# HGRN gate functions regrouped around the tenth projection, and the first mLSTM scores placed ahead of the context states

## The reference, cut to what matters

```python
def _hgrn_gates(f_pre, lb):
    fp = f_pre.astype(jnp.float32)
    logf = jnp.log(lb + (1.0 - lb) * jax.nn.sigmoid(fp))
    k = (1.0 - lb) * jax.nn.sigmoid(-fp)
    return logf, k

# HGRN, per head: q = silu(q), both directions' (logf, k), v; then a chunkwise scan
#   b = cumsum(logf);  attention inside a chunk decays with exp(b_t - b_s)
#   S_new = exp(b_last) * S + (k * exp(b_last - b))^T v
#   out = rms(o) * silu(g)

# mLSTM, per head and direction, over the latents, starting from the context's final state C
#   s = (q k^T) * exp(dlog - m);  h = (w_inter * q C + s v) / max(|den|, exp(-m))
```

## Time and profile before

| what | value |
|---|---|
| median of three runs | 2908.68 us (2907.45 to 2909.07) |
| the profiled execution, its own time | 2908.8 us |
| its span | 2907.0 us |
| PE busy | 2704.5 us (93%) |
| PE weight loads busy | 2196.0 us (76%) |
| DVE busy | 1577.1 us (54%) |
| ACT busy | 1046.3 us (36%) |
| POOL busy | 558.4 us (19%) |
| mean granted clock of PE | 0.95 of full speed |

### The profile page before, as it was taken

One profiled execution on the slowest core, in us unless ns is written; L12 is line 12 of the kernel. 1 busy time (PEld: TensorE's weight loads), 2 busy tenths in 40 slices (PEclk: granted clock), 3 DMA queues, 4 the chain that ended last, 5 costly groups with the idle time before them and its releaser, 6 DMA issues.

```text
span 2907.0 us, 33020 instructions
## 1 busy us (share of the span) xinstructions
PE 2704.5 (93%) x13552; PEld 2196.0 (76%) x13552; DVE 1577.1 (54%) x2304; ACT 1046.3 (36%) x1550; POOL 558.4 (19%) x506
## 2 busy tenths in 40 slices
PE   7999999999998988988999999999788898999998
PEld 4888888878887877965888788887585564588786
DVE  4764445368667676267622554534527875353444
ACT  4212121256566553134422343423222333253333
POOL 0101010116444441000000031310104442021111
PEclk8999999999999999989999999999986789999999
DMA  7444444321111112020222333332211120222221
GB/s 286 166 180 191 152 185 171 137 113 69 48 66 48 48 69 83 23 87 1 102 101 87 132 110 135 143 131 78 90 45 71 60 79 30 87 102 87 95 96 42
DMA packets 44935, 292.66 MB, mean 101 GB/s; under 512 B 4976, under 2 KB 4976, under 8 KB 17904
## 3 DMA queue, kind: packets, MB, share of 16 engines
q1 hardware_dynamic: 42480, 280.06, 26.1%
q10 hardware_dynamic: 2304, 10.49, 0.9%
HBM read 271.65 MB, written 18.87 MB: 100 GB/s over the span
## 4 chain that ended last, share of the span: by engine, by line
PE 81%; DVE 11%; ACT 5%; issue 2%; POOL 1%; DMA 1%; DVEq 0%; SPq 0%; POOLq 0%; another core or an unknown queue 0%; ACTq 0%
PE ps L308 80%; DVE hd L1557 1%; POOL tb L2829 1%; DVE wb L2936 1%; ACT hd L1480 0%; ACT hd L1478 0%; DVE wb L2940 0%; DMA x<-in_x 0%; DVE hd L1559 0%; PE ps L1729 0%; DVE wl L909 0%; DVE x L1581 0%; ACT L1483 0%; ACT L1478 0%; PE ps L3003 0%
## 5 line engine op out<-in xcount | busy, mean ns | idle before, releaser
L308 PE MATMUL ps<-xs,wh 128*128 128x512 f32 (+1 forms) x2816 | 785.1, 366 | 13.7 <-DVE xs L943 13.6
L308 PEld LDWEIGHTS ps<-xs,wh 128*128 128x128 f32 x2816 | 508.2, 190 | 99.0 <-issue 15.7
L308 PE MATMUL ps<-xs,wl 128*128 128x512 f32 (+1 forms) x1408 | 513.0, 364 | 0.0
L308 PE MATMUL ps<-h,wh 128*128 128x512 f32 (+1 forms) x1408 | 391.1, 364 | 7.9 <-POOL h L1141 7.9
L893 DVE TENSOR_TENSOR wl<-w,wh 128x2048 fp32r<-128x2048 f32 (+4 forms) x114 | 246.9, 2167 | 255.9 <-ACT wh L887 255.7
L887 ACT ACTIVATE wh<-w 128x2048 fp32r<-128x2048 f32 (+4 forms) x114 | 203.9, 1789 | 302.0 <-PE ps L308 271.9
L308 PEld LDWEIGHTS ps<-xs,wl 128*128 128x128 f32 x1408 | 267.1, 190 | 42.2
L308 PEld LDWEIGHTS ps<-h,wh 128*128 128x128 f32 x1408 | 253.4, 189 | 51.1 <-POOL h L1141 9.6
L308 PE MATMUL ps<-h,wl 128*128 128x512 f32 (+1 forms) x704 | 255.8, 363 | 0.0
L308 PE MATMUL ps<-x1h,wh 128*128 128x512 f32 x584 | 240.4, 412 | 7.0 <-DVE x1lr L1284 3.9
L308 PE MATMUL ps<-x1h,wl 128*128 128x512 f32 x584 | 236.3, 405 | 0.0
(11 more groups left out here) (436 smaller groups left out, 4834.6 us busy)
## 6 DMA issues: line engine op xcount, KB each, us to landing
w<-in_adat SPq DMA_DIRECT2D x52, 1024.0 KB, 4.9
w<-in_f1i SPq DMA_DIRECT2D x22, 1024.0 KB, 6.6
w<-in_f2i SPq DMA_DIRECT2D x22, 1024.0 KB, 4.8
w<-in_f3i SPq DMA_DIRECT2D x22, 1024.0 KB, 4.8
s_tables<-t ACTq DMA_DIRECT2D x16, 640.0 KB, 3.0
cs<-s_tables SPq DMA_DIRECT2D x16, 640.0 KB, 3.9
w<-in_ada SPq DMA_DIRECT2D x8, 1024.0 KB, 9.1
w<-in_whf SPq DMA_DIRECT2D x8, 1024.0 KB, 4.8
```

The source lines that it names most:

```text
L308: return e.matmul(out, l, r, start=st, stop=sp)
```

## The change

Three things change; no arithmetic is removed or added.

First, a new item `gates h` holds the four forget sigmoids on ACT and the three operations on k on DVE. It stands directly ahead of `fill h, 9`. The two Ln and the four scans move into `fill h, 9`, behind the sigmoids of q and gs and behind the request for the joint table. Second, in the last head `early 0` and `1` move from steps 2 and 3 to 0 and 1, each `drain` moves up one step, and the first value weight of mLSTM, `wmv 0`, is loaded and split inside HGRN's list (split in step 12 of head 7) instead of after it. Third, the scores and the decay of mLSTM's first unit stand ahead of the context's states on PE, its DVE part ahead of the states' copies, and ACT's scan part waits for `uC` instead of the last state.

```diff
-        out = [("fill", 0, 0), ("split", value_key(0, 0))] + [("fill", 0, p) for p in (1, 3, 4, 6, 7, 8, 9, 2, 5)]
-        out += [("split", ("whf", 1, 2048))] + [("v", 0, i) for i in range(6)] + [("prep", 0, n) for n in range(LEAD)]
+        out = [("fill", 0, 0), ("split", value_key(0, 0))] + [("fill", 0, p) for p in (1, 3, 4, 6, 7, 8, 2, 5)]
+        out += [("gates", 0), ("fill", 0, 9), ("split", ("whf", 1, 2048))] + [("v", 0, i) for i in range(6)] + [("prep", 0, n) for n in range(LEAD)]
...
-                        (7, 6): [("split", ("wmq", 1, 2048))]}.get((h, i), [])
-                out += [("early", n) for n in {(7, 2): [0], (7, 3): [1], (7, 4): [2], (7, 6): [3], (7, 8): [4],
+                        (7, 6): [("split", ("wmq", 1, 2048))], (7, 12): [("split", ("wmv", 0, 2048))]}.get((h, i), [])
+                out += [("early", n) for n in {(7, 0): [0], (7, 1): [1], (7, 4): [2], (7, 6): [3], (7, 8): [4],
...
-                out += [("drain", n) for n in {(7, 7): [0], (7, 9): [1], (7, 11): [2], (7, 13): [3]}.get((h, i), [])]
+                out += [("drain", n) for n in {(7, 6): [0], (7, 8): [1], (7, 10): [2], (7, 12): [3]}.get((h, i), [])]
...
-                out += fill if i == 9 else []
+                out += [("gates", h + 1)] + fill if i == 9 and h < 7 else []
...
@@ act_hgrn
                 if p == 9:
                     w.wait_ge(*fA.at(h, "gs", "l"))
                     e.activation(SB[0], z["q"], ACT.Sigmoid).then_inc(*fA.of(h, "sq"))
                     e.activation(SB[1], z["gs"], ACT.Sigmoid).then_inc(*fA.of(h, "sg"))
                     logs(e)
+                    for j in range(2):
+                        e.activation(z[f"b{j}"], z[f"b{j}"], ACT.Ln, scale=olb[:, j, h:h + 1],
+                                     bias=lb[:, j, h:h + 1]).then_inc(*fA.of(h, "ln", j))
+            elif item == "gates":
+                for j in range(2):
+                    e.activation(z[f"k{j}"], z[f"b{j}"], ACT.Sigmoid, scale=-1.0).then_inc(*fA.of(h, "k", j))
+                    w.wait_ge(*fA.at(h, "k", j))
+                    e.activation(z[f"b{j}"], z[f"b{j}"], ACT.Sigmoid).then_inc(*fA.of(h, "b", j))
...
@@ dve_mlstm, ahead of the copies of the context's states
+        dve_decay(e, w, 0)
...
@@ pe_mlstm, behind tc2 and ahead of the wait for kw
+        w.wait_ge(*mlA.at("k", 3))
+        w.wait_ge(*mlV.at("q", 3))
+        ml_scores(e, w, 0)
+        ml_decay(e, w, 0)
...
-        w.wait_ge(*mlV.at("C", 1, 3, 1))
+        w.wait_ge(*mlV.at("uC"))
```

More of the change, by code:

```diff
@@ L1388, in sp_hgrn @@
                         load(e, w, ("wmq", u, 2048), (mlP, "q", 2 * u + 1))
+                    for u in range(2):
+                        load(e, w, ("wmv", u, 2048), (mlP, "v", u, 3))
             elif item == "v":
@@ L1773, in sp_mlstm @@
     def sp_mlstm(e, w):
-        for u in range(2):
-            load(e, w, ("wmv", u, 2048), (mlP, "v", u, 3))
         save_out(e, w, 7)
@@ L2013, in last_exp, with dve_decay @@
         return (n, i, 1 if hi - lo > 128 else 0)
+    def dve_decay(e, w, n):
+        NB, NM = NBM[n % 2]
+        b = banks("dc", n)
+        nm = cst("nmF") if UNIT[n][1] == 0 else cst("nmB")
+        w.wait_ge(*dcP.at(n))
+        if n >= 2:
+            w.wait_ge(*dcA.at(*last_exp(n - 2, 3)))
+        e.tensor_tensor(rows(NM, 4), rows(b, 4), nm.unsqueeze(1).to_broadcast([128, 4, 128]),
+                        ALU.add).then_inc(*dcV.of(n, "m"))
+        e.tensor_copy(NB, b).then_inc(*dcV.of(n, "b"))
     def dve_scan(e, w):
         split_lo1(e, w, MGK[0], mg_hi)
-        for item, n in ML:
+        for item, n in ML[2:]:
             h, j = UNIT[n]
@@ L2020, in dve_scan @@
             if item == "decay":
[L2021 to L2029, removed]
+                dve_decay(e, w, n)
             elif item == "weigh":
@@ L2061, in dve_scan, with ml_scores, ml_decay @@
                                                    op0=ALU.mult, op1=ALU.add).then_inc(*dvV.of(n, hf, "h", t))
+    def ml_scores(e, w, h):
+        PR = slice(64 * (h % 2), 64 * (h % 2) + 64)
+        for i in range(4):
+            b = banks.take(w, "sc", h, i)
+            mm(e, b, kt[PR, h // 2, 128 * i:128 * i + 128], qt[PR, h // 2, :], True, True).then_inc(*sqP.of(h, i))
+    def ml_decay(e, w, n):
+        col = 32 * UNIT[n][1] + UNIT[n][0]
+        b = banks.take(w, "dc", n)
+        mm(e, b, ident[0:64, col:col + 1].to_broadcast([64, 128]), Mr[0:64, :], True, True).then_inc(*dcP.of(n))
+        banks.give(("dc", n), (dcV, n, "b"))
     def pe_scan(e, w):
         w.wait_ge(*mlV.at("C", 1, 3, 1))
-        w.wait_ge(*mlA.at("k", 3))
-        w.wait_ge(*mlV.at("q", 3))
-        for item, n in ML:
+        for item, n in ML[2:]:
             if item == "scores":
[L2069 to L2072, removed]
+                ml_scores(e, w, n)
                 continue
@@ L2077, in pe_scan @@
             if item == "decay":
-                b = banks.take(w, "dc", n)
-                mm(e, b, ident[0:64, col:col + 1].to_broadcast([64, 128]), Mr[0:64, :], True, True).then_inc(*dcP.of(n))
-                banks.give(("dc", n), (dcV, n, "b"))
+                ml_decay(e, w, n)
             elif item == "weigh" and j == 1:
```

50 lines of the change are left out of this document (21 added, 29 removed).

## The result

The changed kernel takes 2871.2 us (median of four runs, 2870.4 to 2872.1), the kernel before, timed beside it, 2908.9 us. The ratio is 0.9871, 95% interval 0.9854 to 0.9888: 37.6 us gained, where 54.8 were forecast. The time is inside the range given, but 17 us above the value and 5 us above the band of 2847 to 2866 us that the forecast itself had. The profiled execution has a span of 2869.2 us, 37.8 less than before.

The account below looks back on a forecast made before the run. PE, busy 93% of the span, was held by seven 6.3 us waits for DVE's KS product and the slowed clock behind them. Gains of 45.5 + 3.1 + 6.2 = 54.8 us from 2908.8 gave 2854 us, range 2840 to 2876.

Parts of the forecast that it names:

- the new stall: Ahead of the next head's first fill, PE waits 2.2 us for DVE in six heads: 13.2 us lost.
- rival 6: A table load holds ACT 2.7 us, not 1.3, ahead of the scans: 16 us more, 2870 us; chance 0.01.
- rivals 2: DVE's backlog paces the head, with a new stall of 4 to 8 us: 2865 to 2889 us; chance 0.12.
- 3: No new stall at all, DVE being 2.2 us quicker than walked: saves 13 us, 2841 us; chance 0.08.
- rival 4: PE's transposes wait on something else ending nearly as late, so little is gained: 2900 to 2910 us; chance 0.02.
- rival 5: Slower kernel: half clock for most of the head behind the stall before each next head's first fill; chance 0.03.
- no fall of the clock in it: PE's clock was to hold through the 2.2 us stall ahead of the next head's first fill, costing nothing extra.
- Rival 1: The new stall also drops the clock, costing 9 to 17 us over six heads: 2863 to 2871 us; chance 0.12.
- The sign of being wrong: A head's period over 55 us would show the forecast wrong; 53 us was expected.
- (a): Last head, early 0 first: early 2 starts at T + 34.5, T ending PE's fill 9; 6.5 us lost.
- (b): Drain 0 one step earlier: PE's 4.07 us wait halves, gaining 2.0 us, plus 1.6 us of low clock.
- (c): Early split of wmv 0 saves 5.6 us of waiting and 2.0 of half clock; 2.0 returns at the ninth bank.

Follow-up runs that it names:

- Experiments 3: Changed kernel with DVE's sel 4 moved between gates and fill 9, ahead of the scans; 2858.3 us.
- 4: Kernel of experiment 3 with the next forget weight's split also moved, directly behind fill 9; 2846.0 us.
- experiment 1: Changed kernel with only its first change kept: early products, drains, first value weight and first scores back as before; 2877.9 us.
- experiment 2: Changed kernel with early 0 and early 1 back in steps 2 and 3 of the last head; 2867.7 us.
- experiment 8: Kernel of experiment 4 with early 0 in step 2, early 1 in step 0 without waiting for rows, gate weight's split two steps earlier; 2843.3 us.
- experiment 12: Kernel of experiment 4 with early 0 and early 1 back in steps 2 and 3 of the last head; 2843.5 us.
- experiment 9: Kernel of experiment 8 with head 7's forget sigmoids, Ln and scans moved into steps 7 and 8 of head 6; 2842.1 us.
- 11: Kernel of experiment 8 with DVE filling the last four of eight low rows with zeros instead of computing them; 2842.3 us.
- experiment 5: Changed kernel with its third change undone: first scores and decay behind the context's states again; 2875.8 us.

## Why the prediction came out 17 us short

Of the 17 us between forecast and result, the rows above put 10.0 on Part 1 (35.5 for 45.5), 5.1 on Part 2 (a loss of 2.0 for a gain of 3.1) and 0.6 on Part 3 (5.6 for 6.2); the 1.3 us given back behind the first output had no term.

**Part 1, removed.** Right. No transpose waits for KS, five table loads a head are two.

**Part 1, the new stall.** Its place and length were right: 2.3 us, in six heads, at `sel 4`, where 2.2 was worked out. The walk through ACT and DVE holds row by row. The timeline of ACT and then of DVE behind fill 9 of head 1, with T = 755.85:

```profile
751.41 1.28 ACT L1490 ACT_TABLE_LOAD   x1
752.70 0.85 ACT L1490 ACTIVATE hd<-hd 128x768 f32<-128x768 f32 x1
...
758.00 1.28 ACT L661 ACT_TABLE_LOAD   x1
759.29 1.95 ACT L1479 ACTIVATE hd<-hd,small 128x768 f32<-128x768 f32 x2
```

```profile
760.36 1.23 DVE L1551 TENSOR_TENSOR_SCAN hd<-cst,hd 128x512 f32<-128x512 f32 x1 [1.57 <-ACT hd L1479]
...
763.59 1.03 DVE L1553 TENSOR_TENSOR_SCAN hd<-cst,hd 128x256 f32<-128x256 f32 x1
...
766.27 2.65 DVE L909 TENSOR_TENSOR wl<-w,wh 128x2048 fp32r<-128x2048 f32 x1
768.84 0.72 DVE L1603 COPY_PREDICATED at<-m,ps 128x512 f32<-128x512 uint8 x1
```

Scans from T + 4.5 (4.6 worked out), `sel 4` from T + 13.0 to 13.7 (13.5). The next function starts 1.29 us after either table load. The Trainium skill, page ScalarE: Activation LUTs, section "What ACT_TABLE_LOAD costs", gives the load itself about 1283 ns, with which these rows agree, and a drain of 1380 ns on top of it, which no row here shows; rival 6 is out. So are rivals 2 and 3 (the stall is 2.3 us, neither 4 to 8 nor nothing), rival 4 (no transpose waits) and rival 5 (the clock is back at 1.00 within 4 us).

**The step that failed: "no fall of the clock in it".** Rival 1 is what happened. The clock fell at all six stalls of 2.3 us: each of the six stretches of 5 us around them has a mean clock of 0.66, which is (1 - 0.66) x 5 = 1.7 us of PE's work. Experiments 3 and 4 show that the stall makes it: at 1.58 us the clock holds, in all six heads, and without a stall there is no low clock from 700 to 1005 us. Six times 1.7 is 10.2 us, and so Part 1 brought 35.5 and not 45.5 us.

The argument behind the step was that PE had stood for longer before its clock fell. In head 1 of the kernel before, PE stopped at 753.7, and its windows are

```profile
754.00:756.00 2.00, 0.00 (x0) 0.00 (x0) 2.00 (x3) 1.99 (x3) 1.80 (x2) 1.00 0.00 0
756.00:758.00 2.00, 0.00 (x0) 0.00 (x0) 2.00 (x4) 2.00 (x5) 2.00 (x3) 0.55 0.00 0
```

The clock fell at about 756.2, so PE had stood for 2.5 us: only 0.3 us more than the new stall's 2.2. In the next head the same stall had lasted 5.3 us before the clock fell (812.3 to 817.6). A moment that moves by 2.8 us from one head to the next gives no bound for a stall of 2.2 us. In the changed kernel the clock fell 2.0 to 2.7 us after PE had stopped, in some heads just before and in some just after it resumed. Nor had the old trace a case to compare with: between 600 and 1290 us no wait of PE is longer than 1.24 and shorter than 2.61 us. A chance of 0.12 for rival 1 was too small for that. The sign of being wrong, a period over 55 us, could not show it either: the clock's 1.7 us on top of the 53 worked out stay below 55, and measured were 54.8.

**Part 2.** Its sum had a gain of 3.1; the rows have a loss of 2.0. By its terms:

(a) Early 2 was to start at T + 34.5 and starts at T + 37.9, so this term cost 9.9 and not 6.5. Early 0 began at T + 16.3, as walked, but DVE needed 4.6 us for four rows beside POOL, 3.0 before the change; there is a second wait of 2.3 us in it, and PE worked at half clock for 4 us from its start and for 3 us more behind the second wait. The Trainium skill, page SBUF — State Buffer, section "Who interferes with whom", has a DVE instruction with two inputs in SBUF contend with a POOL instruction that reads SBUF, and the trace agrees: the four took 1.14 us each with POOL busy throughout, and 0.75 before the change, when POOL was idle for 1.7 of the 3.0 us. Of the 9.9 us, 7.6 are there with the old order too (experiment 1), so they come with the first part, whose gates and scans are late; 2.3 are the early products' new place (experiment 2).

(b) Drain 0's wait halved as forecast, to 1.96, but its low clock stayed, 1.7 us.

(c) `wmv 0` brought 6.8 where 5.6 + 2.0 - 2.0 was worked out; the wait at the ninth bank is 2.1 us and costs no clock in the changed kernel's trace.

These three turn the gain of 3.1 into a loss of 0.7; the other 1.3 us are within what the experiments can resolve and are not attributed. What exactly the last head waits for in its first 30 us is not settled by the experiments. Early 1 put into the wait (8) moved the start of early 2 by 1.3 us against experiment 12, for 2.8 us of work; scans that end 2.6 us sooner (9) and less work on DVE behind the factors (11) moved it by 0.5 us or less. The trace has these in a row there, each behind the other: scans, POOL's subtractions, ACT's Exp, DVE's products, rows. That this chain sets the time is argued and not shown, since no experiment broke it.

**Part 3.** 5.6 us at the first output and 4.6 by experiment 5, for 6.2. The states took 7.2 us for the 6.4 worked out; the first output still waits 3.25 us, the longest in the scan, with 8 us at low clock behind it.

**The parts together.** Undone one by one, the second and third parts' moves give 6.8 + 2.8 + 4.6 - 3.6 = 10.6 us; undone together they give 6.6 (experiment 1). The four differences are each uncertain by 1 to 2 us, and a clock that falls behind a wait of 2 us in one kernel and not in the next moves any of them by 1.7; no run separates the spread from that.

## What to carry to other kernels

A long stall that is taken away can leave a short one, and a short one is priced with its clock: here 2.3 us of waiting cost 4.0, and to shorten it to 1.6 gave three times what was taken off it (2.25 for 0.73). Where the old trace has no wait of the new one's length, the clock's fall is an open case with a large chance, not a detail. When work is made late, ask which of what the in-order queue has behind it could go first: one merge that needed nothing of the scans, and one weight, were worth 25 us here.

## What the runs showed of the hardware

The length of a wait alone doesn't decide whether the granted clock falls. Six of six at 2.3 us fell; none at 1.58. Near 2 us it went both ways in the same place of the program. Behind the wait for drain 0, 1.95 to 1.96 us, the clock fell in the changed kernel and in experiments 3, 4, 8 and 11, and held in 2, 9 and 12. Behind the wait for the ninth value bank, 2.1 us, it fell in 2, 8 and 12, and held in the changed kernel and in 3, 4 and 9. In experiment 8 a wait of 2.89 us inside early 0 had a clock of 0.54 in the 2 us behind it; in experiment 9 the same wait, as long, had none. The timeline and the windows of PE there:

```profile
1030.55 0.50 PE L308 MATMUL ps<-x1h,wh 128*128 128x512 f32 x1 [2.90 <-DVE x1lr L1606]
```

```profile
1026.00:1028.00 2.00, 1.58 (x6) 0.67 (x4) 2.00 (x4) 0.00 (x0) 2.00 (x3) 1.00 0.00 0
1028.00:1030.00 2.00, 0.00 (x0) 0.00 (x0) 2.00 (x3) 0.00 (x0) 1.95 (x3) 1.00 0.00 0
1030.00:1032.00 2.00, 1.45 (x6) 1.22 (x7) 2.00 (x4) 0.00 (x0) 0.00 (x0) 1.00 0.00 0
```

And in the changed kernel's scan the clock fell behind a wait of 1.04 us that follows products of 129 columns:

```profile
1274.34 1.33 PE L308 MATMUL ps<-mr,cst 64*128 64x512 f32 x2 [1.04 <-ACT xc L2013]
```

```profile
1274.00:1276.00 2.00, 1.66 (x4) 0.69 (x5) 1.54 (x7) 0.79 (x4) 0.00 (x0) 0.78 0.00 0
1276.00:1278.00 2.00, 2.00 (x9) 1.77 (x9) 1.86 (x7) 0.00 (x0) 0.00 (x0) 0.50 0.02 4
```

What decides it besides the length was not found. Of two kernels that differ by 2 us, the windows behind each wait of about 2 us therefore have to be read, all of them, before a difference is put down to the edit.
